# Adding fourteen attention rows on GpSimd instead of VectorE, and giving the weight sums of even and odd branch units a semaphore each

## What is computed

```
a      = windowed attention output            # 520 tokens x 1024
b_out  = gated short convolution output       # 520 tokens x 1024
branch_a = a @ w_attn_branch                  # 1024 x 2048
branch_b = b_out @ w_conv_branch              # 1024 x 2048
merged = sigmoid(ga + b_gate[0]) * branch_a + sigmoid(gb + b_gate[1]) * branch_b
x      = x + rmsnorm(merged @ w_o)            # 2048 x 2048
...                                           # feed-forward part and output gate
```

## Time and profile before

| | us |
|---|---|
| median of three runs | 2645.37 (2645.24 to 2646.09) |
| the profiled execution, its own time | 2644.46 |
| its span in the trace | 2642.7 |
| PE busy in the span | 2631.3 (100%) |
| DVE busy | 2265.0 (86%) |
| ACT busy | 1414.1 (54%) |
| POOL busy | 195.2 (7%) |

### The profile page before, as it was taken

One profiled execution on the slowest core, in us unless ns is written; L12 is line 12 of the kernel. 1 busy time (PEld: TensorE's weight loads), 2 busy tenths in 40 slices (PEclk: granted clock), 3 DMA queues, 4 the chain that ended last, 5 costly groups with the idle time before them and its releaser, 6 DMA issues.

```text
span 2642.7 us, 55478 instructions
## 1 busy us (share of the span) xinstructions
PE 2631.3 (100%) x20853; PEld 2571.2 (97%) x20853; DVE 2265.0 (86%) x4000; ACT 1414.1 (54%) x2592; POOL 195.2 (7%) x296
## 2 busy tenths in 40 slices
PE   9999999999999999999999999999999999999999
PEld 8999999999999999999999999999999999999899
DVE  7988888888899987898888888888888768789987
ACT  6544555555566555655555555555555463445454
POOL 0221000000011000000000000000000000000000
PEclk9999999999999999999999999999999999999999
DMA  6676334433487565756566655665569576565774
GB/s 229 186 204 187 133 120 139 136 128 118 160 283 217 170 174 144 266 156 176 168 193 189 189 153 169 188 204 173 157 192 310 152 244 171 162 207 165 246 265 152
DMA packets 162481, 487.12 MB, mean 184 GB/s; under 512 B 17337, under 2 KB 51521, under 8 KB 158928
## 3 DMA queue, kind: packets, MB, share of 16 engines
q1 hardware_dynamic: 129184, 372.41, 40.2%
q0 software_dynamic: 32976, 112.38, 19.4%
q10 hardware_dynamic: 144, 0.15, 0.0%
HBM read 426.42 MB, written 57.30 MB: 183 GB/s over the span
## 4 chain that ended last, share of the span: by engine, by line
PE 66%; DVE 1%; issue 0%; ACT 0%; DVEq 0%; ACTq 0%
PE pair L1218 56%; PE pair L1183 5%; PE pair L1121 2%; PE pair L1317 2%; PE pair L1295 1%; DVE v_lo L1976 0%; DVE lo L2350 0%; PE pair L1078 0%; ACT o_hi L1452 0%; DVE lo_A L2350 0%; PE pair L1272 0%; DVE s_raw L2294 0%; PE pair L1263 0%; DVE lo_E L2350 0%; DVE s_raw L2275 0%
## 5 line engine op out<-in xcount | busy, mean ns | idle before, releaser
L1218 PE MATMUL pair<-o_hi,v_hi 128*128 128x260 f32 x5840 | 1655.9, 284 | 1.2 <-DVE v_lo L1976 0.8
L1218 PE MATMUL pair<-o_hi,v_lo 128*128 128x260 f32 x5840 | 1648.8, 282 | 0.0
L1387 ACT ACTIVATE v_hi<-s_raw 128x512 fp32r<-128x512 f32 (+1 forms) x1384 | 861.9, 626 | 882.9 <-PE pair L1218 797.7
L1218 PE MATMUL pair<-lo,v_hi 128*128 128x260 f32 x4172 | 1178.5, 282 | 0.0
L1976 DVE TENSOR_TENSOR v_lo<-s_raw,v_hi 128x512 fp32r<-128x512 f32 (+1 forms) x1288 | 874.2, 681 | 298.3 <-ACT v_hi L1387 261.0
L1218 PEld LDWEIGHTS pair<-o_hi,v_hi 128*128 128x128 f32 x5840 | 1098.0, 188 | 14.4 <-issue 11.9
L1218 PEld LDWEIGHTS pair<-o_hi,v_lo 128*128 128x128 f32 x5840 | 1099.9, 188 | 0.0
L1218 PEld LDWEIGHTS pair<-lo,v_hi 128*128 128x128 f32 x4172 | 784.1, 188 | 0.2
L1387 ACT ACTIVATE v_hi<-s_one 128x512 fp32r<-128x512 f32 (+1 forms) x228 | 142.3, 627 | 199.7 <-PE pair L1218 163.9
L1218 PE MATMUL pair<-lo_E,v_hi 128*128 128x260 f32 x834 | 236.0, 283 | 0.0
L1218 PE MATMUL pair<-lo_A,v_hi 128*128 128x260 f32 x834 | 235.2, 282 | 0.0
(11 more groups left out here) (301 smaller groups left out, 2595.1 us busy)
## 6 DMA issues: line engine op xcount, KB each, us to landing
s_raw<-in_sstream SPq DMA_DIRECT2D x468, 512.0 KB, 5.0
s_one<-in_sstream POOLq DMA_DIRECT2D x168, 512.0 KB, 5.4
raw<-f_scr SPq DMA_DIRECT2D x12, 1040.0 KB, 7.6
s_raw<-in_sstream SPq DMA_DIRECT2D x32, 384.0 KB, 4.0
g_scr<-d_h SPq DMA_DIRECT2D x16, 520.0 KB, 2.9
g_in<-g_scr SPq DMA_DIRECT2D x32, 260.0 KB, 4.1
x_scr<-y_sb SPq DMA_DIRECT2D x8, 1040.0 KB, 5.5
s_one<-in_sstream POOLq DMA_DIRECT2D x32, 256.0 KB, 4.6
```

The source lines that it names most:

```text
L1218: mm = pe.matmul(out, wt[:, slot, kk * P:kk * P + P], r[:, k, :], start=j in (0, 1, 3) and k == 0 and n == 0, stop=k == nk - 1 and n == 2, ...
L1387: nc.scalar.activation(v_hi[:, n % 4, 0:width], src, ACT.Copy, scale=0.5 if halved(u) else 1.0).then_inc(v_hi_rdy, 1)
```

## The change

Of the sixteen attention rows, fourteen are added to the convolution rows by `tensor_tensor` on POOL (`add_rows`), counted by a new semaphore `merged_pool`. Rows 14 and 15 are still added by DVE. `rows_merged` waits for either count, DVE waits for it before its early operand forms, and ACT before it reuses an `acc` tile. The issue of `s_one`'s DMAs is split in `first_part` and `second_part`, and even and odd units count on semaphores of their own (`s1_pair`). The two late gates move from units 41 and 43 to 42 and 44. In the first unit of the `w_o` product, DVE makes the sum with 9 ahead of two low parts.

```diff
-LATE_GATES = {U_AT + 1: KD - 2, U_AT + 3: KD - 1}
+LATE_GATES = {U_AT + 2: KD - 2, U_AT + 4: KD - 1}
...
         def sum_ready_1(eng, u, h):
-            if by_dma(u):
+            if U_BR <= u < U_O:
+                eng.wait_ge(s1_pair[u % 2], 32 * ((u - U_BR) // 2 + 1))
+            elif by_dma(u):
...
         def rows_merged(eng, rows):
-            eng.wait_ge(merged_ready, rows)
+            eng.wait_ge(merged_pool, min(rows, KD - 2))
+            if rows > KD - 2:
+                eng.wait_ge(merged_ready, rows - KD + 2)
...
# early_unit (first unit of w_o on DVE)
                 o_low(s, 3)
+                if s == 1:
+                    evac(u, 9)
                 v_low(nxt)
                 v_low(nxt + 1)
-                evac(u, 9)
+                if s != 1:
+                    evac(u, 9)
...
# branch_unit on DVE
-                    if j == 1 and u > U_AT:
-                        merge(2 * (u - U_AT) - 1)
...
-                    if j == 6 and u >= U_AT:
-                        merge(2 * (u - U_AT))
+                    if j == 6 and u == U_O - 1:
+                        merge(KD - 2)
...
                     if u == U_AT + 2 and j == 6:
+                        rows_merged(dve, 4)
                         t1(1, 0)
                     if u == U_AT + 4 and j == 6:
+                        rows_merged(dve, KH)
                         t1(1, 1)
                     if u == U_O - 2 and j == 6:
+                        rows_merged(dve, KH + 4)
                         t2(1, 0)
...
# POOL
-            def add_conv_sum(u):
+            def first_part(u):
                 w, h = max(u - 2, U_BR - 1), u % 2
                 c = slice(h * 4 * P, (h + 1) * 4 * P)
                 pool.wait_ge(v_lo_rdy, s_of(w, 1, h) + 1)
                 pool.wait_ge(s2_done, sums_of(w, h))
-                pool.wait_ge(s1_dma, 32 * summed(u - 1))
-                pool.dma_start(s_one[:, c], sstream[r_of(u), 2, :, c]).then_inc(s1_dma, 16)
-                pool.wait_ge(s1_dma, 32 * summed(u) - 16)
-                pool.dma_start(s_one[:, c], sstream[r_of(u), 3, :, c], accum_op=ALU.add).then_inc(s1_dma, 16)
+                pool.dma_start(s_one[:, c], sstream[r_of(u), 2, :, c]).then_inc(s1_pair[h], 16)
+
+            def second_part(u):
+
+                h = u % 2
+                c = slice(h * 4 * P, (h + 1) * 4 * P)
+                pool.wait_ge(s1_pair[h], 32 * ((u - U_BR) // 2) + 16)
+                pool.dma_start(s_one[:, c], sstream[r_of(u), 3, :, c], accum_op=ALU.add).then_inc(s1_pair[h], 16)
...
+            def add_rows(u):
+
+                for m in (2 * (u - U_AT), 2 * (u - U_AT) + 1):
+                    pool.wait_ge(br_free, GATE_AT[KD + m] + 1)
+                    pool.tensor_tensor(x_tile(m), x_tile(m), two(acc[u % 4][:, m % 2, :]), ALU.add)\
+                        .then_inc(merged_pool, 1)
+
+            first_part(U_BR + 4)
             for u in range(U_BR + 4, U_O):
-                add_conv_sum(u)
+                second_part(u)
+                if u - 3 >= U_AT:
+                    add_rows(u - 3)
+                if u + 1 < U_O:
+                    first_part(u + 1)
+            add_rows(U_O - 3)
+            add_rows(U_O - 2)
```

More of the change, by code:

```diff
@@ L388, in summed @@
         def summed(u):
-            return sum(by_dma(w) for w in range(u + 1))
+            return sum(by_dma(w) for w in range(u + 1) if not U_BR <= w < U_O)
         def sum_ready_1(eng, u, h):
-            if by_dma(u):
+            if U_BR <= u < U_O:
+                eng.wait_ge(s1_pair[u % 2], 32 * ((u - U_BR) // 2 + 1))
+            elif by_dma(u):
                 eng.wait_ge(s1_dma, 32 * summed(u))
@@ L559, in build @@
         af_stored = sem("af_stored")
+        merged_pool = sem("merged_pool")
         br_hi_rdy = sem("br_hi_rdy")
@@ L569, in build @@
         s1_dma = sem("s1_dma")
+        s1_pair = [sem(f"s1_pair{i}") for i in range(2)]
         s2_done = sem("s2_done")
@@ L1753, in branch_unit @@
                         if u >= U_AT + 4:
-                            act.wait_ge(merged_ready, 2 * (u - U_AT - 3))
+                            rows_merged(act, 2 * (u - U_AT - 3))
                         copied(u, 0, d11, r1_out)
@@ L3219, in _ @@
                 if n == 14:
-                    add_conv_sum(U_BR)
-                    add_conv_sum(U_BR + 1)
+                    first_part(U_BR)
+                    first_part(U_BR + 1)
+                    second_part(U_BR)
+                    second_part(U_BR + 1)
                 if n % 4 == 3:
@@ L3224, in _ @@
                     if w == 3:
-                        add_conv_sum(U_BR + 2)
-                        add_conv_sum(U_BR + 3)
+                        first_part(U_BR + 2)
+                        second_part(U_BR + 2)
+                        first_part(U_BR + 3)
+                        second_part(U_BR + 3)
                     pool.wait_ge(af_rdy, 4 * w + 4)
```

## The result

The changed kernel takes 2654.27 us (median of 7 runs, 2653.37 to 2655.44), the kernel before 2645.24 (7 runs, 2643.5 to 2646.09). The ratio is 1.0034, with a 95% interval of 1.0025 to 1.0044: 9 us slower. The time lies above the range of the prediction, 2639.6 to 2648.9, on the side of rival B.

What follows compares the result with a forecast made beforehand. PE bounds the kernel, stalling for late sums of a full DVE; -1.3 (unit 40) - 0.3 (convolution half) - 1.0 (early sum) + 0 (adds) = -2.6 us, 2642.8 against the median; range 2639.6 to 2648.9.

Steps and rivals of the forecast that it cites:

- rival B: Product 6's start, units 41 to 46: POOL and DVE fully exclude each other; +3.5 us, 2648.9; chance 0.28.
- x: What one POOL add costs DVE in time: taken as 0.61 us, between 0 and the add's length, 1.08.
- The length of an add: POOL add of an attention row: estimated as two passes, 1.08 us, between bounds of 0.54 and 1.6.
- 13 (x - 0.61): Attention units, DVE full: cost of moving the merges; -2.6 us at most, 0 in the middle, +6.1 at 1.08.
- point of decision, 0.81: Attention units: the value of x from which rival B decides; below it the kernel is no slower.
- The early sum: First w_o unit: the sum with 9 ahead of two low parts gains 0.65 to 1.1 us, taken as 1.0.
- The late gates and the new waits of DVE: Attention units: moved gates keep their price of 0.61, and DVE's waits before its three forms cost 0 us.
- the weight sums: Two semaphores end DVE's waits for s_one: 1.3 us gained in unit 40, 0.3 in the convolution half.
- Case A: Units 41 to 45: POOL and DVE don't disturb each other, 2.6 us more won; -5.2 us, 2640.2; chance 0.24.
- Rival C: Weight sums: semaphores do nothing, another wait holds s_one as long; -1.0 us is left, 2644.4; chance 0.08.

Runs made afterwards that it cites:

- e10_rows_apart: The changed kernel with the even row's POOL add ahead of second_part and the odd row's behind it; 2650.65 us, ratio to the kernel before 1.0022.
- e7_spare_add: e2_rows_on_dve plus fourteen POOL adds on spare tiles that nobody waits for; 2663.44 us, ratio to the kernel before 1.0067.
- e2_rows_on_dve: The changed kernel with all sixteen rows added by DVE again, semaphores, moved gates and early sum kept; 2642.04 us, ratio to the kernel before 0.9988.
- e1_sems: The kernel before with only the weight sums' two semaphores added; 2643.35 us, ratio to the kernel before 0.9992.
- e9_no_read: The changed kernel with a POOL memset of the acc tile in place of each add, leaving fourteen additions out; 2641.24 us, ratio to before 0.9983.
- e4_rows_by_dma: The changed kernel with each of the fourteen POOL adds replaced by an accumulating DMA issued from POOL; 2652.30 us, ratio to before 1.0026.

## Why the prediction was wrong, point by point

**The step that failed** is "This middle value, x = 0.61, is what I take", with the reason given for it, that the adds fall half on sums and waits. They don't. An add waits for the gate of its row, and it starts right behind it (in `e10_rows_apart` the gate ends at 842.51 and the add starts at 842.60) or behind `second_part`, and in both places DVE's next instructions are low parts, gates or stream sums, with two SBUF inputs each; in the changed kernel not one of the fourteen adds runs beside a sum. Measured, x is 1.1 for an add by itself (1.7 once) and 1.3 to 1.5 in a back-to-back pair; the mean in the changed kernel is 18.4 / 14 = 1.31. The hope was too high even where adds do fall on sums: in `e7_spare_add` six do, and each still costs 0.77. The arithmetic of that step doesn't give 0.61 either: 1.08 - 1.2 / 2 is 0.48, and 0.61 was chosen as "about what the merge itself cost", which set the term to zero.

**The length of an add** was put at 1.08 us, between the bounds 0.54 and 1.6. The record of a single add, 1.69, is longer, but it holds a wait for the instruction that DVE has under way: in `e7_spare_add` this one ends at 897.86 and the add at 899.02, 1.16 us later. So for an add by itself the 1.08 was near, and so was the 1.13 us that the prediction worked out from the Trainium skill, "GPSIMD Engine Reference", section 3.1; DVE loses 1.12. Too low it was for a pair: in the changed kernel's pairs the first takes 1.60, the second ends some 1.26 us behind it, and DVE loses 2.6 to 3.0.

**The sum with the right x.** Against `e2_rows_on_dve`, DVE is busy for 9.6 us more in the branch half (90.94 against 81.30), near the 18.4 - 14 x 0.61 = 9.9 that adds and merges come to, and idle for 0.8 more, mostly in four short waits for ACT's high parts at 835, 847, 871 and 873. PE's half is 93.7 - 83.26 = 10.4 longer. The two agree, as they must where DVE is the bound. The form 13 (x - 0.61) of the prediction gives 9.1 with the measured x: it lacks the fourteenth add and these waits. Rival B's point of decision, 0.81, was passed by far. B's price of +6.1 us was mis-sized by x, 1.08 where it was 1.31 in the mean, and by the same two omissions.

**The whole account**, in the profiled executions: -2.5 us (semaphores, moved gates and early sum, `e2_rows_on_dve`), +10.4 (adds, branch half), and about +0.5 where PE now waits 0.94 us ahead of the second product of the `w_o` operand (0.46 in `e2_rows_on_dve`). That is +8.4, and the first split matmul of `w_o` is indeed late by 8.4 (939.20 against 930.83). The last 1.0 us of the span's 9.4 arises at about 2370, far from the change, where the records show two short waits of PE for DVE, 0.6 us in all; I did not test it, and its cause is open.

**The parts that were right in the sum.** Without POOL's adds the forecast was -2.6 us; the profiled execution of `e2_rows_on_dve` shows -2.5, the medians -3.6. The early sum was put at 1.0: from the last branch matmul to the first split one it takes 26.34 us in `e1_sems` and 25.41 in `e2_rows_on_dve`, 0.9 less. The wait for `y_sb` is gone from the first `w_o` unit. The waits for `s_one` are gone from 730 to 950. The late gates and the new waits of DVE cost nothing that a row shows.

**Right in size, wrong in place: the weight sums.** I put 1.3 us of their gain on unit 40. Its stall hardly shrank (1.07 us against 1.13 in the earlier trace rows), and the unit became 0.3 shorter; the rest came in units 41 and 43 (0.7 and 0.5). The 0.3 that I put on the convolution half is there in the changed kernel, whose half takes 81.34 us against 81.68; in `e1_sems` unit 39 is 0.3 shorter too, but unit 32 loses 0.5 in short waits of PE, and unit 40 starts at 819.85 as before. DVE's timeline in the changed kernel tells why unit 40's stall stayed:

```profile
823.97 0.69 DVE L1979 SCALAR_TENSOR_TENSOR v_lo<-s_raw,v_hi 128x512 fp32r<-128x512 f32 x1 [1.06 <-ACT v_hi L1393]
824.58 1.24 DVE L2249 TENSOR_TENSOR af_lo<-af_raw,af_hi 128x1040 fp32r<-128x1040 f32 x1
...
826.94 1.23 DVE L2249 TENSOR_TENSOR af_lo<-af_raw,af_hi 128x1040 fp32r<-128x1040 f32 x1
828.09 0.42 DVE L2583 TENSOR_TENSOR acc<-pair,acc 128x260 f32<-128x260 f32 x1
828.43 0.68 DVE L1979 SCALAR_TENSOR_TENSOR v_lo<-s_raw,v_hi 128x512 fp32r<-128x512 f32 x1
829.03 0.42 DVE L2587 TENSOR_TENSOR acc<-pair,acc 128x260 f32<-128x260 f32 x1
```

DVE came to the unit earlier, and then waited 1.06 us for ACT's high part (0.16 at this place in the kernel before). The wait for a DMA had turned into a wait for ACT, with the same work behind it up to the sum. The prediction saw that DVE was busy "almost without a gap" behind the late `s_one`, but not which engine would be next in line.

**The rivals.** Case A's arithmetic is borne out by `e9_no_read`: the stalls of units 41 to 45 vanish, and the time is 3.8 us lower in the profiled executions and 4.4 in the medians, against 5.2, of which unit 40 was to give 1.3 and gave 0.3. Its condition, adds that don't disturb DVE, is false. Rival C, that the semaphores do nothing, is false by the trace: the waits are gone and three units are shorter; by its time alone `e1_sems` can't be told from no change. Rival B's mechanism was the true one, and the rule of the Trainium skill quoted for it was to be believed against the hope of gaps: the 0.28 that I gave it was far too low for a DVE that is full, whose work all round the adds reads two SBUF tiles. B's range was too low as well, since the range of the whole ended at its 2648.9, at x = 1.08. (Its lower end, "2639.6", is not the 2639.3 that was worked out for A; nothing hangs on it.)

## What to carry to other kernels

Moving an elementwise add from a full DVE to POOL frees DVE of one instruction's pace (0.61 us here) and takes from it POOL's own length (1.1 to 1.5 us), wherever DVE's neighbouring instructions read two SBUF tiles; count the price of the move in the engine's time that is freed, and read the neighbours' inputs in the timeline before hoping for gaps. Work that only writes (a memset) cost DVE nothing here. An accumulating DMA left DVE alone too, but its result was there only 3.7 to 13.2 us after its issue, 8 in the middle. Where two halves of a buffer come free apart, give each its own semaphore; and when a wait is taken away, look for the engine that is late next, since the gain may fall in another place.

The fastest kernel that computes everything is `e2_rows_on_dve`: two semaphores, early sum, rows on DVE, 2642.04 us, 0.9988 of the kernel before (0.9979 to 0.9997).

## What the runs showed of the hardware

The engine that has to wait isn't only delayed by one instruction: POOL's pair of adds took 6.11 us in `e7_spare_add`, of which 3.2 passed before DVE's first sum let it in, and 2.86 in the changed kernel. A full DVE can so hold POOL, and all behind it in POOL's queue, for several of its own instructions.

PE's granted clock was 0.50, its 1.2 GHz level, for the first 3.3 us of unit 45 in the changed kernel, behind units with stalls of up to 2.1 us. In `e9_no_read` and `e10_rows_apart`, with stalls of 1.3 at most, it was 1.00 throughout the attention units; but so it was in `e7_spare_add`, with stalls of up to 1.96, so the longest stall alone doesn't tell. Sixteen matmuls of unit 45 start 0.22 us apart instead of 0.12, about 1.6 us of loss, but they bring little on top: DVE is busy for 12.23 of the unit's 12.30 us, and units 43 and 44 take as long at full clock. Where PE had nothing else to wait for, the price shows: in `e4_rows_by_dma` the clock was 0.50 for 3.4 us from 860.7 on, behind a stall of 4.5 us, and unit 43 took 16.2 us, 1.6 more than its 10.1 and the stall.
